# A decoder layer on one core: the state space without a stage of its own, its work placed in the first SwiGLU and between the units of the projection

## The reference

```python
x = x + 0.5 * swiglu(rmsnorm(x), w1_gate, w1_up, w1_down)
h = rmsnorm(x)
q, k, v, qi, ki, wi, u, gates = split(h @ w_in)      # one combined projection
a = sparse attention: scores = sum_head wi * relu(qi . ki); the 256 best causal keys of a query; softmax over them
s = glu(gelu(s5(u) + d_skip * u))                    # the state space
x = x + merge(sigmoid(gates), a @ w_pa, s @ w_pb) @ w_out
x = x + 0.5 * swiglu(rmsnorm(x), w2_gate, w2_up, w2_down);  y = rmsnorm(x)
# s5: ab = exp(dt*A) (complex), x_t = ab * x_(t-1) + bb @ u_t, y_t = Re(C @ x_t);
# 32 groups of 16 channels with 64 complex states each; outputs are also the states after the last token and the samples' new states
```

## Time and profile before

| | us |
|---|---|
| median of 3 runs | 3033.44 (3024.99 to 3033.66) |
| the profiled execution | 3033.91 |
| its span in the trace | 3032.1 |
| input and first SwiGLU | 0 to 835 |
| projection until the index scores | 835 to 876 |
| index scores | 876 to 917 |
| rest of the projection (DVE selects) | 917 to 1319 |
| attention | 1319 to 1767.7 |
| state space | 1767.7 to 2037.2 |
| output, second SwiGLU, final norm | 2037.2 to 3032 |
| PE busy, whole span | 2741.1 (90%) |
| DVE, ACT, POOL busy | 1318.2, 664.7, 818.6 |

### The profile page before, as it was taken

How to read it: one execution, slowest core, us unless ns; L and a number is a source line. 1 busy time by engine, 2 the same in 40 slices (tenths; PEclk the granted TensorE clock), 3 DMA queues, 4 the chain that set the end, 5 groups by cost and what they waited for, 6 DMA issues and landing times.

```text
span 3032.1 us, 38694 instructions
## 1 busy us (share of the span) xinstructions
PE 2741.1 (90%) x16047; PEld 2489.3 (82%) x16047; DVE 1318.2 (43%) x2743; ACT 664.7 (22%) x1182; POOL 818.6 (27%) x521
## 2 busy tenths in 40 slices
PE   6999999999989999957689945859999999999998
PEld 4999999999868999944443534639989999999998
DVE  4122222222628999968842255134561222222225
ACT  5111111110333332213333431041131111111113
POOL 5422232232321111232500025003443223323220
PEclk8999999999979999976679656579999999999999
DMA  3211111110112322232223021025211111111101
GB/s 126 70 42 42 43 57 55 42 56 25 63 28 63 98 79 96 84 133 83 93 76 137 1 41 16 0 82 182 85 35 56 43 42 53 59 43 52 46 15 57
DMA packets 182811, 189.72 MB, mean 63 GB/s; under 512 B 18524, under 2 KB 164176, under 8 KB 179784
## 3 DMA queue, kind: packets, MB, share of 16 engines
q1 hardware_dynamic: 162568, 133.17, 14.6%
q0 software_dynamic: 2944, 35.65, 3.2%
q10 hardware_dynamic: 17136, 18.53, 1.8%
HBM read 160.10 MB, written 25.78 MB: 61 GB/s over the span
## 4 chain that ended last, share of the span: by engine, by line
PE 68%; DVE 18%; issue 7%; ACT 2%; DMA 2%; POOL 1%; SPq 1%; DVEq 0%; ACTq 0%; POOLq 0%
PE ps L240 33%; PE ps L249 16%; PE ps L1835 3%; PE ps L1818 2%; PE ps L1216 2%; PE ps L820 2%; DVE x_T L752 2%; DVE k_index_T_high L1133 1%; PE ps L842 1%; DVE new_small L1131 1%; PE ps L1527 1%; PE ps L98 1%; PE ps L653 1%; DVE probs L866 1%; PE ps L603 1%
## 5 line engine op out<-in xcount | busy, mean ns | idle before, releaser
L240 PE MATMUL ps<-normed_split,f_weights_split 128*128 128x344 f32 x6336 | 1001.8, 320 | 0.0
L240 PEld LDWEIGHTS ps<-normed_split,f_weights_split 128*128 128x128 f32 x6336 | 998.6, 188 | 0.7 <-issue 0.2
L249 PE MATMUL ps<-f_hidden_split,f_down_split 128*128 128x344 f32 x2880 | 456.6, 319 | 0.0
L249 PEld LDWEIGHTS ps<-f_hidden_split,f_down_split 128*128 128x128 f32 x2880 | 453.9, 188 | 0.0
L293 DVE TENSOR_TENSOR f_hidden<-f_silu,ps 128x344 f32<-128x344 f32 x132 | 67.7, 513 | 858.9 <-PE ps L240 850.5
L603 PE MATMUL ps<-normed_split,in_weights_split 128*128 128x344 f32 (+1 forms) x2520 | 403.6, 321 | 7.3 <-POOL normed_split L129 6.1
L603 PEld LDWEIGHTS ps<-normed_split,in_weights_split 128*128 128x128 f32 (+1 forms) x2520 | 396.3, 187 | 11.2 <-POOL normed_split L129 6.5
L303 DVE SCALAR_TENSOR_TENSOR x_T<-ps,x_T 128x344 f32<-128x344 f32 x480 | 248.0, 517 | 196.9 <-PE ps L249 196.9
L209 POOL TENSOR_TENSOR f_hidden_split<-f_hidden,f_hidden_split 128x344 fp32r<-128x344 f32 x132 | 122.7, 930 | 569.4 <-DVE f_hidden_split L296 569.4
L201 POOL TENSOR_TENSOR f_weights_split<-f_weights_raw,f_weights_split 128x1024 fp32r<-128x1024 f32 x88 | 210.8, 2419 | 0.0
L177 ACT ACTIVATE f_silu<-ps 128x344 f32<-128x344 f32 x132 | 59.9, 455 | 650.4 <-PE ps L240 650.4
(11 more groups left out here) (299 smaller groups left out, 2803.9 us busy)
## 6 DMA issues: line engine op xcount, KB each, us to landing
f_weights_raw<-in_w_gate SPq DMA_DIRECT2D x44, 512.0 KB, 3.9
f_weights_raw<-in_w_up SPq DMA_DIRECT2D x44, 512.0 KB, 4.0
f_down_raw<-in_w_down SPq DMA_DIRECT2D x44, 512.0 KB, 3.7
in_weights_raw<-in_w_in SPq DMA_DIRECT2D x34, 512.0 KB, 3.8
gates_T<-projected ACTq DMA_DIRECT2D x16, 516.0 KB, 2.6
gates<-gates_T SPq DMA_DIRECT2D x16, 516.0 KB, 4.4
x_meanwhile<-x_T SPq DMA_DIRECT2D x1, 4128.0 KB, 12.0
x_T<-x_meanwhile SPq DMA_DIRECT2D x1, 4128.0 KB, 17.2
```

The source lines that it names most:

```text
L240: mm = nc.tensor.matmul(m.ps[:, NCH * half + c, :CH], m.wh[:, 2 * e + half, a, k * P:(k + 1) * P], m.xn[:, k, b, cols(c)], start=(k == 0 a ...
L249: mm = nc.tensor.matmul(m.ps[:, bank, :CH], w[:, e, a, o * P:(o + 1) * P], m.hh[:, (2 * p + e) % 4, b, cols(c)], start=(e == 0 and t == 0) ...
```

## The change

The stage of the state space and its barrier go. Its parts are placed elsewhere:

- **In the first SwiGLU**: hooks (`beside`) in `ffn_sp`, `ffn_act`, `ffn_pe` and `ffn_dve`. ACT issues ten parameter loads (`par_load`) behind the four loads of the gains at the very start, and two more in the norm. PE's parameter transposes follow the first two gate and up products. DVE makes the parameters after products 0, 1, 2, 4 and 6, and, in POOL's place, the rotation table, a quarter each after products 8, 10, 12 and 14; SP writes each quarter to memory (`rotations_meanwhile`).
- **Between the projection's units**: the new table `SLOTS`. u comes first, so that the state space's slots (QL, KZ, BX, Y, YT, YS, YST, SOS, GLU) stand between units. Chunk states are made after QL1, KZ0, ki and KZ1. q, k and v come last. u goes through memory (two stores, eight loads a unit), and so do the kernel's columns; `d_skip` comes in as 32 more small matmuls in KZ. DVE runs `ssm_dve` (its matrices, then for each quarter of the states 6 products, 8 scans, 6 products) between the norm and the selection. The GLU's product (four of 128x1032) is POOL's, and the result is stored (`state_space_branch`).
- **In the attention**: SP loads that result, ACT copies it in four of the late steps (`AT_OB`), POOL subtracts.
- **The gathers** of the indexer keys leave the start of POOL's program and stand behind the slot of gate unit 9; the page arithmetic that they need follows the first norm on DVE.

```diff
-GROUPS = (("ki", C_KI, IDX + IDX_HEADS, 1), ("qi", C_QI, P, 2), ("q", C_Q, P, 4), ("k", C_K, P, 4),
-          ("v", C_V, P, 4), ("u", C_U, P, 4), ("g", C_G, P, 2 * KD - 2),
-          ("g_last", C_G + (2 * KD - 2) * P, P, 2))
...
+SLOTS = ([("u", 0), ("u", 1), ("QL", 0), ("u", 2), ("QL", 1), ("u", 3), ("QL", 2), ("KZ", 0), ("ki", 0), ("KZ", 1),
+          ("g", 0), ("qi", 0), ("KZ", 2), ("qi", 1), ("KZ", 3), ("BX", 0), ("g", 1), ("Y", 0), ("g", 2), ("YT", 0),
+          ("g", 3), ("Y", 1), ("g", 4), ("YT", 1), ("g", 5), ("Y", 2), ("g", 6), ("YT", 2), ("g", 7), ("Y", 3),
+          ("g", 8), ("YS", 0), ("YT", 3), ("g", 9), ("YST", 0), ("g", 10), ("SOS", 0), ("GLU", 0), ("g", 11), ("SOS", 1),
+          ("GLU", 1), ("g", 12), ("SOS", 2), ("GLU", 2), ("g", 13), ("GLU", 3)]
+         + [("g", j) for j in (14, 15)] + [(name, j) for name in ("v", "k", "q") for j in range(4)])
...
+    for v, x in enumerate(SLOTS):
+        if v >= 2:
+            pe.wait_ge(s.ev, NCH * (v - 1))
...
+        if x in (("QL", 1), ("KZ", 0), ("ki", 0), ("KZ", 1)):
+            states((("QL", 1), ("KZ", 0), ("ki", 0), ("KZ", 1)).index(x))
+        if x == ("KZ", 3):
+            pe.wait_ge(s_ssm.s_read, NQ)
+            turn(("ki", 0))
+            index_weights()
+        if x == ("g", 1):
+            scores()
...
+        if x == ("g", 9):
+            pool.wait_ge(s.mm, done_slot(("Y", 3)))
+            for b in range(TS):
+                smp_load(pool, m, b, m.kidx[:, b], i.cache_kidx, s_io.ki_in)
+        if x[0] == "GLU":
+            pool.wait_ge(s.ev, NCH * (v + 1))
+            t = m.tmp[:, TMP_OF[x], :]
+            G.tensor_tensor(t, t, m.yT[x[1]], ALU.mult).then_inc(s.gate, 1)
...
+AT_OB = tuple(range(AT_OUT + 10, AT_OUT + 22, 3))
...
+            act.wait_ge(s_ssm.ob_in, 16)
+            nc.scalar.activation(m.xn[:, 4 + j, 0, :], m.x[:, j, :], ACT.Copy).then_inc(s_ssm.ob_hi, 1)
```

More of the change, by code:

```diff
@@ L160, in ffn_sp @@
         down(p)
+        beside(p)
 def ffn_act_split(nc, act, m, s, f, half):
@@ L278, in ffn_pe @@
         gate_up(f)
+        beside(f)
         if f % 2 and f > 1:
@@ L430, in mix_memory @@
     m.prob = sb("probs", [P, 2, TP])
[L433 to L445, removed]
@@ new lines @@
+MIX_SEMS = ("hi", "lo", "mm", "ev", "tr", "tev", "ki_copied", "wi_T", "wi", "smp_T", "smp_out", "dots", "relu",
+            "score", "chain", "steps", "sent0", "sent1", "dram", "bcast", "rows", "turned", "taken", "link", "raw0", "raw1",
+            "gate")
+SSM_SEMS = ("p_in", "ldt_in", "ldt", "p_T", "c", "d", "a", "e_q", "e_out", "e_in0", "e_in1", "q_built", "w_built",
+            "u_in0", "u_in1", "u_in2", "u_in3", "s_mm", "s_read", "z", "kz_out", "zero", "m_in", "xs", "wg", "st_out", "ob_in",
+            "ob_hi")
@@ new lines, in sample_inputs, with outputs @@
+    def sample_inputs(v, bank):
+        act.wait_ge(s.mm, NCH * (v + 1))
+        A(m.bxs[:].rearrange("p n i t -> p (n i t)"), m.ps[:, bank, :2 * NI * TS], ACT.Copy).then_inc(s.ev, NCH)
+    def outputs(j, v, bank):
+        act.wait_ge(s.mm, NCH * (v + 1))
+        if j == 0:
+            act.wait_ge(s.dram, 32)
+        y = m.stage[:].rearrange("p t (i e c) -> p e i t c", e=2, c=GC)
+        for e in range(2):
+            A(y[:, e], m.ps[:, bank + e, :].rearrange("p (i t c) -> p i t c", i=QI, t=L),
+              ACT.Gelu_apprx_tanh).then_inc(s.ev, 1 + e)
@@ L593, in unit, with mid_pe @@
+def mid_pe(nc, pe, m, s, s_norm, s_ssm):
+    mm = nc.tensor.matmul
+    tr = nc.tensor.transpose
+    def unit(x, v, bank):
+        name, j = x
+        u = UNITS.index(x)
+        width = WIDTH[name]
         pe.wait_ge(s.lo, u + 1)
-        if not (static and u < 2):
-            pe.wait_ge(s.ev, NCH * (u - 1))
-        if name == "q":
-            pe.wait_ge(s.relu, IDX_HEADS * (NB - 2))
         for c in range(NCH):
-            if name == "ki":
+            if c == 2 and v >= 2 and SLOTS[v - 2] in TURNS[1:]:
+                pe.wait_ge(s.tev, 3 * (TURNS.index(SLOTS[v - 2]) + 1))
+            if u == 0:
@@ new lines, in glu @@
+    def glu(j, bank):
+        if j == 0:
+            pe.wait_ge(s_ssm.wg, 32)
+            pe.wait_ge(s.ev, done_slot(("YST", 0)))
+        for c in range(NCH):
+            for k in range(4):
+                y = mm(m.ps[:, bank + c, :CH], m.wgl[:, k, j * P:(j + 1) * P], m.yT[k][:, cols(c)],
+                       start=(k == 0), stop=(k == 3))
+            y.then_inc(s.mm, 1)
+    last = None
+    for v, x in enumerate(SLOTS):
+        name, j = x
+        bank = 3 * (v % 2)
+        if v >= 2:
+            pe.wait_ge(s.ev, NCH * (v - 1))
+        if x in UNITS:
+            unit(x, v, bank)
+        elif name == "QL":
+            inputs_to_states(j, bank)
+        elif name == "KZ":
+            kernel_columns(j, bank)
+        elif name == "BX":
+            sample_inputs(bank)
+        elif name == "Y":
+            outputs(j, bank)
+        elif name == "YT":
+            outputs_turned(j, v, bank)
+        elif name == "YS":
+            sample_outputs(bank)
+        elif name == "YST":
+            sample_outputs_turned(bank)
+        elif name == "SOS":
+            sample_states(j, bank)
+        elif name == "GLU":
+            glu(j, bank)
+        if last:
+            turn(last)
+        last = x if name in ("v", "k", "q") else None
+        if x in (("QL", 1), ("KZ", 0), ("ki", 0), ("KZ", 1)):
+            states((("QL", 1), ("KZ", 0), ("ki", 0), ("KZ", 1)).index(x))
+        if x == ("KZ", 3):
+            pe.wait_ge(s_ssm.s_read, NQ)
+            turn(("ki", 0))
+            index_weights()
+        if x == ("g", 1):
+            scores()
```

1329 lines of the change are left out of this document (690 added, 639 removed).

## The result

The changed kernel takes 2882.06 us (median of 4, 2878.97 to 2882.43) against 3033.55 us of the kernel before: a ratio of 0.9499 (95% interval 0.9484 to 0.9514). The forecast was 2902, with a range of 2864 to 2945.

A forecast was written before the change was run, and what follows sets the result against it. PE bounds the first SwiGLU, DVE's chain the rest of the projection, nobody the state space stage. Terms -1 + 4 + 119 + 10 + 6 - 269.6 = -131.6 took the span from 3032.1 to 2900.5, time 2902 us, range 2864 to 2945.

The forecast's parts named there:

- The sign: Whole kernel: the change was forecast to make it faster, with a chance of 0.97; same 0.01, slower 0.02.
- B: First SwiGLU: PE has no gap, so its added parameter transposes are paid in full, +4 us (1 to 6).
- F: The state space stage and its barrier, up to the output stage's first load: removed, -269.6 us.
- C: From the end of the projection's first unit to the first index scores: more PE work, +119 us (104 to 135).
- D: From the scores to the projection's end: DVE's chain unchanged, POOL's added work lengthening it, +10 us (0 to +22).
- E: Attention: ACT's four copies and POOL's four subtractions add +6 us (2 to 14).
- the full-clock rival: Everything at full clock and the start gained: C 104, D 0, E 4, A -8; -165.6, time 2868; chance 0.15.
- the case that PE paces: Within D: PE's list, some 415 us against DVE's 402 + 6, sets the pace, giving +22.
- the row at 1920: Profile row of the kernel before: 20.00 us of continuous PE work at clock 0.50, cited against the full-clock rival.
- A: Start: gain from POOL's eight gathers leaving against ten parameter loads issued first by ACT, -1 us (-8 to +10).

## Why the prediction was right, point by point

The sign, the range and the mechanism held: 269.6 us of a stage in which nobody was busy went, and work on PE came back where PE sets the pace, ahead of the scores. B came out to 0.2 us; F could not do otherwise. Three terms were mis-sized, two of them in the direction of the gain. That the sum missed by no more than 19.9 us is in part luck: the start, B, the first unit and the end came out 14.2 us above what the sum has, and C, the scores, D and E together 34.1 below. The measured 2882 stands at the lowest edge of the forecast's own 2882 to 2922, and the full-clock rival's 2868 is nearer to it than my 2902.

**D, 17 us off, is the largest.** That DVE's chain "does not change" was the step that failed. I counted what POOL was given, four products and the gathers at +6, and not what left the stretch with the units: nine units stand ahead of the scores instead of three, and take their weight splits along. POOL's work beside DVE's chain, before:

```profile
L579 POOL TENSOR_TENSOR in_weights_split<-in_weights_raw,in_weights_split 128x1024 fp32r<-128x1024 f32 x31 | 76.0, 2452 | 351.9 <-ACT in_weights_split L480 351.9
```

and after:

```profile
L990 POOL TENSOR_TENSOR in_weights_split<-in_weights_raw,in_weights_split 128x1024 fp32r<-128x1024 f32 x25 | 61.6, 2464 | 280.3 <-ACT in_weights_split L787 280.3
L1593 POOL DMA_INDIRECT past_k_index<-in_cache_kidx,page_rows x8 | 7.9, 992 | 7.6 <-issue 7.6
L1013 POOL TENSOR_TENSOR projected<-projected,y_T 128x1032 f32<-128x1032 f32 x3 | 7.2, 2412 | 36.2 <-ACT projected L933 36.2
L1013 POOL TENSOR_TENSOR projected<-projected,y_T_last 128x1032 f32<-128x1032 f32 x1 | 2.4, 2416 | 11.9 <-ACT projected L933 11.9
```

DVE's busy time there fell by 6.9 us (377.84 to 370.90), its idle time stayed at 24: that is the whole of the -7.0. Two large operations fewer, at the 1.4 to 1.5 us measured for each, would give only -3. The rest shows when each of DVE's 986 operations is set against its shortest time in seven of these traces. What they took above that lies, but for 1.7 us at most, in those that overlap a split or a product of POOL: 55.9 us beside the 31 splits of before (1.8 each), 40.5 beside the 25 of now (1.6 each), 8.1 beside the four products, under 0.1 beside the gathers. I also added 4 for the case that PE paces. It did not: PE waited 5.01 us for DVE at the end. The tie was as close as I wrote: with late loads that wait was 0.35 us, and without the products PE did end last.

**C, 11 us off.** I took the middle between full and half clock. KZ and the states ran at 1.00, so +104 was the better end (its terms add up to 130.8, not 131.2, which changes nothing), and 4.4 us above it remain. BX alone is more than that: I halved it to 3.5, and it took 7.0 at 0.50, with 2.6 more in the unit behind it. Half was not exact either: the tripled output slots took 44.9 us at 0.50 and 25.4 at 1.00, which is 1.8 times, not twice. The outputs at 1.00 also belong to the rival "everything at full clock", whose C and D were nearer than mine; its start was not. The rival was given 0.15 because of the row at 1920. That row was read wrongly: I took the clock of 0.50 to belong to those matmuls, when they had come in at it, behind a wait of 15.1 us for DVE, and kept it. The runs with the outputs tripled show both: out of a unit they ran at 1.00, behind a wait of 3.3 us at 0.50. The Trainium skill (TensorE: Matmul & The Clock Gate, "What's actually happening") says that activity releases the throttle; for these fp32 matmuls the trace does not agree, since 35.00 of 35 busy us stayed at 0.50 in the run with the wait.

**A, 9.4 us off, inside its range.** The row of the one load that held SP for 6.93 us was the right row, but I took it for one load; the hold of ACT was 5.79 and 13.63. The load that took 13.63 us to issue here took 1.29 us on SP's queue in the run with late loads, and the one of the same size ahead of it 0.86 on ACT's. What x and the weights, moving at that moment, have to do with it was not tested. The gathers gave back 4.6, not 8.

**Not foreseen**: the first unit's 3.8 us, of which 2.5 came back when DVE waited before its build of large products; and the end of the attention, in which a clock that may or may not come back decides over 15 to 26 us, more than any term but C and F. **E** was put at 6 and is 2.6, between traces that both have the end of the attention at 0.50; with the build's wait, which leaves the attention as it is, it took 447.5, less than before, so 2.6 is no more than its scatter. At 0.50 PE is busy for 59.45 of 60 us at the end of the attention, so ACT's copies and POOL's subtractions lie beside it.

## What to carry to other kernels

Work of a stage without a bound is worth moving between units of a stage that has one; before you carry a row's duration over, look at what stood ahead of it. Here the outputs, which had run at 0.50 behind a wait, ran at 1.00 between units; BX and most often the first slot behind the scores did not. When units move from one stretch to another, count everything that goes with them on the other engines, here POOL's splits beside DVE's chain. Loads that nobody needs yet do not belong on the queue of an engine that has the first work of the program to do: issuing one held ACT for 13.63 us.

## What the runs showed of the hardware

The same fp32 matmuls ran at 1.00 for 24 of 24 us when they came out of a unit, and at 0.50 for 35 of 35 when PE had waited 3.33 us ahead of them: there, PE's being busy did not bring the clock back. It did not hold it up everywhere either: Y0 began at 1.00 behind the scores and fell within 3 us, with PE busy, in the run with the waits. In the 8-column products the clock fell from a start without a wait (6.14 us at a mean of 0.59, and 4.38 at 0.87), and the unit behind them took 14 us both times. In the block of one-column ones the mean fell to 0.55, after which the small matmuls of the attention stayed at 0.50 for 60 us in the changed kernel and came back to 1.00 within 4 us in the run with late loads:

```profile
1801.00:1805.00 4.00, 4.00 (x14) 2.58 (x14) 1.44 (x8) 1.59 (x4) 0.00 (x0) 0.50 0.53 132
1805.00:1835.00 30.00, 26.76 (x135) 14.99 (x134) 14.22 (x69) 25.86 (x69) 4.27 (x2) 0.99 0.13 54
```

What decides between the two is open; the end of the attention went both ways in executions of one kernel. Beside a chain of short operations on DVE, POOL's weight splits of 2.4 us lengthened those operations by 1.6 to 1.8 us for each split; its gathers, 0.99 us each, by nothing that shows.
